# State outputs written as single-value transfers in the middle of a one-core decoder step

## The chip, the core and the metric

One NeuronCore of one Trainium2 chip runs the whole program. The metric is the device time of one execution in microseconds (us), lower is better. Everything is float32 from outside. Inside, each large product is made of three passes over operands split into a high and a low part of TensorE's fast float32 format (fp32r).

## The reference

The program computes one step of a two-branch decoder layer for a prompt of 1024 tokens and 8 single-token samples (1032 columns together):

```python
xn = rms_norm(x, norm_mix)
h, gate_b_in, gate_c_in, u, gate_a, gate_s = jnp.split(xn @ w_in, SPLITS, axis=-1)
conv_y, new_conv_buf = causal_dwconv(gate_c_in * h, conv_buf, conv_a_w, conv_a_b)
z_a = (gate_b_in * conv_y) @ w_out_a
ssm_y, new_re, new_im = s5_mimo(u, s_re, s_im, ...)
ssm_y = jax.nn.gelu(ssm_y)
z_b = (ssm_y @ w_glu_a) * jax.nn.sigmoid(ssm_y @ w_glu_b)
x = x + (jax.nn.sigmoid(gate_a) * z_a + jax.nn.sigmoid(gate_s) * z_b) @ w_o
up_a, up_b = jnp.split(rms_norm(x, norm_ffn) @ w_up, 2, axis=-1)
up_a, new_ffn_buf = causal_dwconv(up_a, ffn_buf, ffn_conv_w, ffn_conv_b)
x = x + (jax.nn.gelu(up_a) * up_b) @ w_down
x = x + jax.nn.sigmoid(rms_norm(x, norm_ple) @ w_ple_gate) * (p @ w_ple)
```

The outputs are `y` (final RMSNorm of `x`, prompt and samples) and the new states: the last two convolution inputs of both convolutions (512 and 2816 channels) and the real and imaginary SSM state (32 groups of 64 values), each for the prompt and for the 8 samples. The model width is 1024, the feed-forward width 2816.

## The kernel before, in words

**Layout.** Activations lie transposed: a tile is 128 channels on the partitions by 1032 tokens. `XT` holds the residual `x` (8 tiles), `XH` and `XL` its scaled high and low parts. A product of one output tile is 72 matmuls of 128x128 by 344 columns: 8 input tiles, 3 passes (`WH`*`XH`, `WH`*`XL`, `WL`*`XH`), 3 column chunks, all in one half of PSUM (`set3(n)` is 3 banks). PSUM banks 6 and 7 are for small work (`bank`, `misc`).

**Staging of weights.** SP loads a 512 KB block into one of two slots of `WST` (`load`, L414) once the split of the block before in that slot is done. ACT copies it to `WH` (`hi`, its engine line is L719), POOL subtracts to `WL` (`lo`, L642), PE waits for `s_wl` (`group`). `hi` waits until PE has finished with the slot's former block.

**Engine programs.** Each engine has an order written out by hand, with semaphores between them; nothing schedules them. In order of time: the start turns `x` (`x_turn`, PE transposes at L1716 into banks 6 and 7, `x_evict` on ACT and DVE) and computes the token norms (`inverse_roots`, `rs_turns` L1754, `rs_evict` L1168); then the projection of `u` (`u_chunk`, `u_product`), the first convolution and the state-space scan; `gate`/`out_a` rounds; eight linear-unit rounds (`glu`, loop at L938 on ACT, each 22.7 us of PE); eight output products (`w_o`, L1496 on DVE adds to `XT`); eleven feed-forward rounds (68 us each); eight rounds of the per-layer embedding (`ple`); the final norm and the output transposes (`out_turn`, L2115).

**States.** DVE leaves the last convolution inputs in `LAST` (128 channels x 26 tiles x 10 values: 2 of the prompt, 8 of the samples; L1402 and L1507) and the SSM state in `FS` (128 x 2 x 16 x 9). Before the change they go out near the end: PE turns them with 58 transposes (`states_out`, L2050 and L2054) in 15 groups, ACT evicts each group to `OST` or `SST`, and SP writes these rows out (L602 to L611).

**End of the feed-forward part.** `down(N_DOWN_END, ...)` adds the last products to `XT` (L1527). DVE has just before that computed `PLW`, the low part of `w_ple` (L1585, L1586). For each new `XT` tile ACT makes `XH` and a square, POOL adds the squares into `RS` (L705), DVE makes `XL` (`split_lo`, L1213). PE runs `product_lo_last` (L1954), in its middle `sum_squares` (L1700: 3 matmuls by a block of ones, which leave every token's sum on all 128 partitions). ACT takes the root of 128x1032 (`rms(2, N_P7)`), DVE the reciprocal (`recip(2)`, L1285), then `ple` scales the first gate product (L1598).

## Time and profile before

| | us |
|---|---|
| three timed executions | 1576.7, 1578.64, 1578.82 |
| their median | 1578.64 |
| the profiled execution | 1578.6 |
| its span in the trace | 1576.8 |
| PE busy in it | 1546.9 (98%) |
| DVE, ACT, POOL busy | 732.8, 418.8, 376.1 |

The profile is one execution. Its span is first to last instruction; 1.8 us lie around it. Matmuls overlap in the pipe, so a matmul's duration is longer than the distance between two of them.

### The profile page before, as it was taken

The numbers are of one execution on the slowest core, as the hardware profiler recorded it, in microseconds if no ns is written. First come the engines' busy times: TensorE is split into PE (matmuls) and PEld (weight loads), VectorE is DVE, ScalarE is ACT, GpSimd is POOL, SyncE is SP. The second block draws the span as 40 slices with busy tenths as digits, with TensorE's granted clock in tenths as the row PEclk, the third lists the DMA queues.
The fourth block names the chain that finished last, engine by engine and source line by source line (L and its number), as shares of the span: only waits on it lengthen the run. The fifth ranks groups of instructions, "written<-read, shape, count | busy, mean of one in ns | idle before, by whom it ended". The sixth has DMA issues, their size and how long they took to land.

```text
span 1576.8 us, 23730 instructions
## 1 busy us (share of the span) xinstructions
PE 1546.9 (98%) x9955; PEld 1528.3 (97%) x9955; DVE 732.8 (46%) x780; ACT 418.8 (27%) x467; POOL 376.1 (24%) x159
## 2 busy tenths in 40 slices
PE   7999999999999999999999999999999999999998
PEld 6899998999999999999999999999999999988998
DVE  4997796233322322245343443534344353458234
ACT  6213212332323222332112121211211112145334
POOL 1121211121212224432213031121313212135241
PEclk9999999999999999999999999999999999999999
DMA  6623617432111103332111020210202111010202
GB/s 183 212 73 102 108 45 190 113 97 79 40 54 53 40 28 120 93 95 81 50 29 57 23 80 2 77 53 27 67 13 80 35 44 53 27 54 0 59 20 108
DMA packets 166499, 108.99 MB, mean 69 GB/s; under 512 B 19217, under 2 KB 158141, under 8 KB 166383
## 3 DMA queue, kind: packets, MB, share of 16 engines
q1 hardware_dynamic: 159794, 99.73, 22.7%
q10 hardware_dynamic: 6656, 8.57, 1.6%
q8 instruction: 36, 0.59, 0.2%
q14 instruction: 13, 0.10, 0.0%
HBM read 89.69 MB, written 17.51 MB: 68 GB/s over the span
## 4 chain that ended last, share of the span: by engine, by line
PE 85%; DVE 9%; DMA 2%; ACT 2%; SPq 1%; issue 1%; ACTq 0%; DVEq 0%
PE PS L1680 60%; PE PS L1980 16%; PE PS L1899 3%; PE PS L1954 1%; DMA sscr<-S 1%; PE PS L2082 1%; SPq L475 1%; PE PS L1852 1%; SPq L463 1%; PE PS L2115 1%; PE PS L1716 0%; PE PS L1842 0%; PE PS L1728 0%; DMA XN<-in_x_prompt 0%; DVE AP L1270 0%
## 5 line engine op out<-in xcount | busy, mean ns | idle before, releaser
L642 POOL TENSOR_TENSOR WL<-WST,WH 128x1024 fp32r<-128x1024 f32 x108 | 266.4, 2467 | 1026.6 <-ACT WH L719 1026.6
L1680 PE MATMUL PS<-XH,WH 128*128 128x344 f32 x1824 | 388.6, 321 | 1.9 <-POOL WL L642 1.3
L1680 PE MATMUL PS<-XL,WH 128*128 128x344 f32 x1824 | 387.0, 320 | 0.0
L1680 PE MATMUL PS<-XH,WL 128*128 128x344 f32 x1824 | 385.0, 319 | 0.0
L1680 PEld LDWEIGHTS PS<-XH,WH 128*128 128x128 f32 x1824 | 305.8, 188 | 2.9 <-POOL WL L642 1.6
L1680 PEld LDWEIGHTS PS<-XL,WH 128*128 128x128 f32 x1824 | 308.5, 189 | 0.0
L1680 PEld LDWEIGHTS PS<-XH,WL 128*128 128x128 f32 x1824 | 304.0, 188 | 0.0
L719 ACT ACTIVATE WH<-WST 128x1024 fp32r<-128x1024 f32 x108 | 110.2, 1021 | 309.0 <-PE PS L1680 238.1
L1527 DVE TENSOR_TENSOR XT<-PS,XT 128x1032 f32<-128x1032 f32 x88 | 108.1, 1230 | 83.0 <-PE PS L1980 83.0
L1980 PE MATMUL PS<-GH,DHW 128*128 128x344 f32 x516 | 110.5, 323 | 3.0 <-DVE XT L1527 3.0
L1980 PE MATMUL PS<-GH,DLW 128*128 128x344 f32 x516 | 109.6, 321 | 0.0
L1980 PE MATMUL PS<-GL,DHW 128*128 128x344 f32 x516 | 109.5, 320 | 0.0
L719 ACT ACTIVATE GH<-TC 128x1032 fp32r<-128x1032 f32 (+1 forms) x24 | 23.9, 994 | 269.6 <-DVE TC L1519 266.5
L1980 PEld LDWEIGHTS PS<-GH,DHW 128*128 128x128 f32 x516 | 86.6, 189 | 3.6 <-DVE XT L1527 3.6
L1505 DVE TENSOR_TENSOR TA<-PS,RS 128x1032 f32<-128x1032 f32 x22 | 27.1, 1232 | 133.8 <-PE PS L1680 133.8
L1290 DVE TENSOR_TENSOR TC<-PS,RS 128x1032 f32<-128x1032 f32 x21 | 25.9, 1232 | 133.1 <-PE PS L1680 133.1
L1980 PEld LDWEIGHTS PS<-GL,DHW 128*128 128x128 f32 x516 | 86.9, 189 | 0.0
L1980 PEld LDWEIGHTS PS<-GH,DLW 128*128 128x128 f32 x516 | 86.7, 190 | 0.0
L719 ACT ACTIVATE TB<-TB 128x1032 f32<-128x1032 f32 x22 | 23.5, 1067 | 124.0 <-DVE TB L1392 124.0
L719 ACT ACTIVATE TB<-TA,KV 128x1032 f32<-128x1032 f32 x22 | 27.6, 1255 | 103.2 <-DVE LAST L1507 103.2
L719 ACT ACTIVATE XH<-XT,KV 128x384 fp32r<-128x384 f32 (+3 forms) x40 | 30.2, 806 | 80.1 <-DVE XT L1496 65.1
L688 POOL TENSOR_TENSOR DLW<-DST,DHW 128x2048 fp32r<-128x2048 f32 x11 | 50.7, 4613 | 0.0
(327 smaller groups left out, 1917.7 us busy)
## 6 DMA issues: line engine op xcount, KB each, us to landing
WST<-in_w_up SPq DMA_DIRECT2D x44, 512.0 KB, 3.9
WST<-in_w_in SPq DMA_DIRECT2D x32, 512.0 KB, 4.5
DST<-in_w_down SPq DMA_DIRECT2D x11, 1024.0 KB, 5.0
xscr<-XT SPq DMA_DIRECT2D x1, 4128.0 KB, 18.4
WST<-in_w_o SPq DMA_DIRECT2D x8, 512.0 KB, 4.4
WST<-in_w_ple_gate SPq DMA_DIRECT2D x8, 512.0 KB, 4.5
out_y_prompt<-OUTT SPq DMA_DIRECT2D x8, 512.0 KB, 2.9
XN<-in_x_prompt ACTq DMA_DIRECT2D x6, 512.0 KB, 8.4
```

Source lines behind the costliest of these rows:

```text
L463: sp.dma_start(U[r * HG:(r + 1) * HG, :, NB:NB + NC], src[:, :, i * NC:(i + 1) * NC]).then_inc(s_ul[q], 16)
L475: sp.dma_start(rows, sscr[q, two * NS:(two + 1) * NS, :, c, :]).then_inc(s_sc[q], 16)
L642: nc.gpsimd.tensor_tensor(WL[:, w], WST[:, slot, 0:tiles * P], WH[:, w].bitcast(F32), ALU.subtract).then_inc(s_wl, 1)
L688: nc.gpsimd.tensor_tensor(DLW[:, :], DST[:, :, :].rearrange("p f n -> p (f n)"), DHW[:, :].bitcast(F32), ALU.subtract).then_inc(s_dl, 1)
L719: copy = lambda o, i, f=ACT.Copy, **k: nc.scalar.activation(o, i, f, **k)
L1290: tt(v3(o), set3(n), v3(RS[:, :]), ALU.mult).then_inc(s_ev, 1)
L1505: tt(v3(TA[:, :]), set3(n), v3(RS[:, :]), ALU.mult).then_inc(s_ev, 1)
L1527: tt(xm, set3(n + m), xm, ALU.add).then_inc(s_ev, 1)
L1680: last = mm(PS[:, 3 * (n % 2) + c, 0:TN], ww[:, w], xx[:, cols], start=(k == 0 and r == 0), stop=(k == ks - 1 and r == 2))
L1852: last = mm(b[two * NS:(two + 1) * NS, c * UC:(c + 1) * UC], W1[:, c, 4 * q + j, two * NS:(two + 1) * NS], UU[q][:, 2 * j + two, 0:UC], st ...
L1899: last = mm(PS[:, 3 * (n % 2) + c, 0:TN], ww[:, w], x[:, c * TN:(c + 1) * TN], start=(k == 0 and r == 0), stop=(k == CT - 1 and r == 2))
L1980: last = mm(PS[:, 3 * (n % 2) + c, 0:TN], ww[:, w], xx[:, k * T + c * TN:k * T + (c + 1) * TN], start=(k == 0 and r == 0), stop=(k == 1 an ...
```

## The change

The new states leave SBUF without a transpose, from ACT's DMA queue, one 4-byte value per piece: `dst` has the channel as its slowest dimension. In each of the eight linear-unit rounds and of the eight output products ACT issues four transfers of SSM state (`states_out(j)`: 128, 1024, 128 and 1024 values); between the two loops, eight transfers of the first convolution (four times 256 and 1024 values); in each feed-forward round four transfers (two times 256 and 1024), and four more after the last one. Together 116 transfers with 70,144 values. The transposes, their evictions and the row writes near the end are gone; two copies of old states within memory stay on SP, behind the load of gate block 3.

Four more edits go with it:

- at the start `x_turn` alternates between banks 6, 7 and banks 2, 5 (`xbank`), so that turn t waits for the eviction of t-2 instead of t-1;
- `inverse_roots()` stands on DVE before the second range-reduction part instead of behind all of them;
- the two `PLW` subtractions come after the additions of down products 1 and 2 instead of before product 0;
- the norm of the last part: `sum_squares` becomes `token_squares` (9 matmuls of one column: 128 tokens on partitions), ACT takes roots of 128x8 and 8x1, DVE reciprocals of the same, PE turns them out to all partitions (`root_turns`, 9 transposes), DVE copies them to `RS`. PE no longer waits for ACT's root before `down_out`. SP's load of the final gain `GFC` is issued before gate block 3 and not behind the state writes.

```diff
+            def states_out(j):
+                for c, part in enumerate(("re", "im")):
+                    for name, cols in ((f"ssm_{part}_p", slice(0, 1)), (f"ssm_{part}_s", slice(1, NB + 1))):
+                        dst = out[name][0].rearrange("b g p -> b (g p)").rearrange("b (j n) -> n j b", n=P)
+                        act.dma_start(dst[:, bass.ds(j, 1), :], FS[:, c, bass.ds(j, 1), cols],
+                                      allow_slow_non_contiguous=True).then_inc(s_so, 16)
+            def last_out(which, f, tile0):
+                for src, cols in ((out[which + "_p"][0, 0], slice(0, 2)), (out[which + "_s"][0, :, 1, :], slice(2, NB + 2))):
+                    rows = src.rearrange("k (f n) -> n f k", n=P)
+                    act.dma_start(rows[:, bass.ds(f, 1), :], LAST[:, bass.ds(tile0, 1), cols],
+                                  allow_slow_non_contiguous=True).then_inc(s_so, 16)
...
                     copy(tile(TH, i * 2 + j), TA[:, :]).then_inc(s_th, 1)
+                    states_out(i * 2 + j)
+
+            for q in range(CT):
+                last_out("conv_a", q, q)
...
                     split_hi(None, tile(XT, m), m, KV[:, bass.ds(m + K_FFN, 1)], TC, i * 2 + (j + 1))
+                    states_out(i * 2 + (j + DT))
...
                 conv_tap(p * 2 + 1)
+                for j in range(2):
+                    last_out("ffn", p * 2 + j, p * 2 + (CT + j))
...
             conv_tap(FT - 1)
+            for f in (FT - 2, FT - 1):
+                last_out("ffn", f, f + CT)
...
-            rms(2, N_P7)
+            act.wait_ge(s_nm, 2)
+            sums = PS[:, 3 * ((N_P7 + 1) % 2), :]
+            copy(SSQ[:, 0, 0:DT], sums[:, 0:DT], ACT.Sqrt, bias=EP[:, :], scale=1.0 / D)
+            copy(SSQ[0:NB, 0, DT:DT + 1], sums[0:NB, DT:DT + 1], ACT.Sqrt, bias=EP[0:NB, :], scale=1.0 / D).then_inc(s_rt, 1)
             hi(G_P7L, 0, N_PW0)
-            for k in range(15):
-                states_out(k)
...
+            if c == 1:
+                inverse_roots()
...
-            dve.wait_ge(s_dh, FP + 1)
-            tt(PLW[:, 0:D], DST[:, 0, :], PHW[:, 0:D].bitcast(F32), ALU.subtract)
-            tt(PLW[:, D:], DST[:, 1, :], PHW[:, D:].bitcast(F32), ALU.subtract).then_inc(s_dl, 1)
             for m in range(DT + 3):
                 if m < DT:
                     down(N_DOWN_END, N_DOWN_END, (m,))
+                if m == 1:
+                    dve.wait_ge(s_dh, FP + 1)
+                    tt(PLW[:, 0:D], DST[:, 0, :], PHW[:, 0:D].bitcast(F32), ALU.subtract)
+                if m == 2:
+                    tt(PLW[:, D:], DST[:, 1, :], PHW[:, D:].bitcast(F32), ALU.subtract).then_inc(s_dl, 1)
...
-            recip(2)
+            dve.wait_ge(s_rt, 2)
+            nc.vector.reciprocal(SSQ[0:NB, 1, DT:DT + 1], SSQ[0:NB, 0, DT:DT + 1])
+            nc.vector.reciprocal(SSQ[:, 1, 0:DT], SSQ[:, 0, 0:DT]).then_inc(s_r7, 1)
+            dve.wait_ge(s_t7, 1)
+            nc.vector.tensor_copy(RS[:, 0:SEQ].rearrange("p (a b) -> p a b", a=2), PS[:, 6:8, :])
+            nc.vector.tensor_copy(RS[:, SEQ:T], PS[:, 3 * (N_P7 % 2) + 2, 400:400 + NB]).then_inc(s_t7, 1)
+            dve.wait_ge(s_t7, 2)
...
-            for k in range(8):
-                states_out(k)
-            rms_read(2)
+            root_turns(N_P7)
             pe.wait_ge(s_dl, FP + 1)
             down_out(N_PW0, N_PW0, 0, PH, PL, PHW, PLW)
-            for k in range(8, 15):
-                states_out(k)
```

**ACT, end of a linear-unit round** (`TH` is the high part of the round's result; the rows behind it are the next round's start or the loop's end). Before:

```order
L719 ACTIVATE TB<-PS 128x1032 [waits s_tf,s_po]
L948 REGISTER_ALU
L719 ISA [waits s_tf]
L719 ACTIVATE TH<-TA 128x1032
L938 REGISTER_ALU
L938 COMPARE_AND_BRANCH
L951 UNCONDITIONAL_BRANCH
L951 ISA
L726 ISA [waits s_stage1]
L719 ACTIVATE WH<-WST 128x1024 [waits s_po]
```

Changed:

```order
L716 ACTIVATE TH<-TA 128x1032
L907 ISA
L907 DMA out_ssm_re_p<-FS 128x1
L907 ISA
L907 DMA out_ssm_re_s<-FS 128x8x1
L907 ISA
L907 DMA out_ssm_im_p<-FS 128x1
L907 ISA
L907 DMA out_ssm_im_s<-FS 128x8x1
L951 REGISTER_ALU
L951 COMPARE_AND_BRANCH
L914 DMA out_conv_a_p<-LAST 128x2x1
```

Four transfers with a register instruction each now stand between the `TH` copy and the next weight copy `WH<-WST`; behind the loop eight more follow (one of them shown) before the `WH<-WST` of the output products.

**PE, from the last low-part matmuls of the first gate product to the second gate product.** Before (the last two groups of the first eight, then `down_out`):

```order
L2050 MATMUL PS<-IDN,LAST 10x128 [waits s_mf]
L2050 MATMUL PS<-IDN,LAST 10x128
L2054 MATMUL PS<-IDN,FS 9x128 [waits s_mf]
L2054 MATMUL PS<-IDN,FS 9x128 x3
L1980 MATMUL PS<-PH,PHW 128x344 [waits s_ev,s_dl,s_rt]
L1980 MATMUL PS<-PH,PHW 128x344 x2
L1980 MATMUL PS<-PL,PHW 128x344 x3
L1980 MATMUL PS<-PH,PLW 128x344 x3
```

Changed:

```order
L1998 MATMUL PS<-XL,WH 128x344 x2
L1745 MATMUL PS<-IDN,SSQ 128x128 [waits s_r7,s_mf]
L1745 MATMUL PS<-IDN,SSQ 128x128 x7
L1747 MATMUL PS<-IDN,SSQ 128x8
L2024 MATMUL PS<-PH,PHW 128x344 [waits s_ev,s_dl]
L2024 MATMUL PS<-PH,PHW 128x344 x2
L2024 MATMUL PS<-PL,PHW 128x344 x3
```

The small transposes of `LAST` and `FS`, each group of which waits for an eviction, are gone; nine transposes of the roots stand in their place, and the wait for `s_rt` has become one for `s_r7`.

**DVE, the end of the feed-forward part.** Before:

```order
L1581 TENSOR_TENSOR TC<-TC,TB 128x344 [waits s_ge,s_ev]
L1583 TENSOR_TENSOR GL<-TC,GH 128x344 [waits s_gh]
L1585 TENSOR_TENSOR PLW<-DST,PHW 128x1024 [waits s_dh]
L1586 TENSOR_TENSOR PLW<-DST,PHW 128x1024
L1527 TENSOR_TENSOR XT<-PS,XT 128x1032 [waits s_po] x4
L1213 SCALAR_TENSOR_TENSOR XL<-XT,KV,XH 128x1032 [waits s_xh]
L1527 TENSOR_TENSOR XT<-PS,XT 128x1032 [waits s_po]
```

Changed:

```order
L1598 TENSOR_TENSOR TC<-TC,TB 128x344 [waits s_ge,s_ev]
L1600 TENSOR_TENSOR GL<-TC,GH 128x344 [waits s_gh]
L1544 TENSOR_TENSOR XT<-PS,XT 128x1032 [waits s_po] x2
L1606 TENSOR_TENSOR PLW<-DST,PHW 128x1024 [waits s_dh]
L1544 TENSOR_TENSOR XT<-PS,XT 128x1032 [waits s_po]
L1608 TENSOR_TENSOR PLW<-DST,PHW 128x1024
L1544 TENSOR_TENSOR XT<-PS,XT 128x1032 [waits s_po]
L1230 SCALAR_TENSOR_TENSOR XL<-XT,KV,XH 128x1032 [waits s_xh]
```

The additions to `XT` of down products 0 and 1 no longer stand behind the two `PLW` subtractions.

## Rows read from the trace of the kernel before

**Rows 1.** The page, part 1: busy time, share, instructions.

```profile
PE 1546.9 (98%) x9955; PEld 1528.3 (97%) x9955; DVE 732.8 (46%) x780; ACT 418.8 (27%) x467; POOL 376.1 (24%) x159
```

**Rows 2.** Chain of waits, 1350 to 1577: start, us, what.

```profile
1410.62 3.32 DVE PLW L1586
...
1434.93 9.65 PE PS L1954 x60
1444.59 1.73 PE PS L1700 x6
1446.32 1.91 PE PS L1954 x12
...
1453.54 2.83 PE PS L1980 x18
...
1460.64 11.36 PE PS L1680 x72
...
1556.34 0.11 PE PS L2102 x2
...
1557.57 0.94 PE PS L2115 x8
```

**Rows 3.** PE's timeline: start, us, what, [idle before, releaser].

```profile
1415.14 0.74 PE L1980 MATMUL PS<-GH,DHW 128*128 128x344 f32 x3 [2.71 <-DVE XT L1527]
```

**Rows 4.** Stretches: us; PE, PEld, DVE, ACT, POOL; granted clock, DMA share, GB/s.

```profile
1416.00:1418.00 2.00, 2.00 (x10) 2.00 (x9) 0.23 (x1) 2.00 (x3) 0.00 (x0) 0.55 0.00 0
1420.00:1422.00 2.00, 2.00 (x15) 2.00 (x14) 1.05 (x1) 0.92 (x1) 1.72 (x1) 1.00 0.00 0
```

**Rows 5.** PE's timeline, the start.

```profile
36.36 0.87 PE L1716 MATMUL PS<-IDN,XS 8*128 8x8 f32 x8 [0.33 <-ACT XT L719]
...
47.53 1.09 PE L1754 MATMUL PS<-IDN,SSQ 128*128 128x128 f32 x8 [1.75 <-DVE SSQ L1164]
```

**Rows 6.** Chain of waits at the start.

```profile
48.22 1.29 DVE RS L1168 x2
```

**Rows 7.** Timeline of a linear-unit round, then of the change to the output products.

```profile
451.51 1.07 ACT L719 ACTIVATE TH<-TA 128x1032 f32 x1 [8.63 <-DVE TA L1485]
...
455.03 2.40 POOL L642 TENSOR_TENSOR WL<-WST,WH 128x1024 fp32r<-128x1024 f32 x1 [15.31 <-ACT WH L719]
...
458.67 0.63 PE L1680 MATMUL PS<-YGH,WH 128*128 128x344 f32 x3
...
587.63 1.07 ACT L719 ACTIVATE TH<-TA 128x1032 f32 x1 [8.63 <-DVE TA L1485]
...
589.73 2.58 POOL L642 TENSOR_TENSOR WL<-WST,WH 128x1024 fp32r<-128x1024 f32 x1 [12.99 <-ACT WH L719]
...
595.10 1.23 DVE L1496 TENSOR_TENSOR XT<-PS,TA 128x1032 f32 x1 [5.04 <-PE PS L1680]
```

**Rows 8.** DVE's timeline behind the feed-forward part.

```profile
1431.26 2.43 DVE L1213 SCALAR_TENSOR_TENSOR XL<-XT,KV,XH 128x1032 fp32r<-128x1032 f32 x1
...
1447.51 6.60 DVE L1285 RECIPROCAL RS<-RS 128x1032 f32<-128x1032 f32 x1 [1.16 <-ACT RS L719]
```

**Rows 9.** The `GFC` load (1024 values): its issue, and the DMA view of 1469.0 to 1470.85.

```profile
1468.76 0.41 SPq L613 DMA_DIRECT2D GFC<-in_norm_final  x1
...
DMA packets 1107, 0.04 MB, mean 21 GB/s; under 512 B 1040, under 2 KB 1107, under 8 KB 1107
...
q1 hardware_dynamic: 1107, 0.04, 37.0%
```

**Rows 10.** Issue durations of one line: min/median/max ns (L510: 1024 pieces of 512 B).

```profile
L778 ACTq DMA_DIRECT2D uscr<-US x4: 455/826/1365, 52.4 to 91.2; - x4
...
L510 SPq DMA_DIRECT2D WC<-w2scr x4: 1817/2183/2565, 182.1 to 188.6; - x4
```

**Rows 11.** ACT's timeline near 52: engine work and a DMA issue.

```profile
51.95 1.06 ACT L719 ACTIVATE WH<-WST 128x1024 fp32r<-128x1024 f32 x1 [5.02 <-PE PS L1728]
52.03 0.38 ACTq L777 DMA_DIRECT2D uscr<-TA  x1
```

More of the change, by code:

```diff
@@ L153, in decoder_step @@
         SQA = at("SQA", [P, T], B0)
-        GFC = at("GFC", [P, DT], B0 + TB4)
-        RT = at("RT", [P, 2, 12], B0 + TB4 + 32)
+        GFC = at("GFC", [P, DT], E0 + 4 * TB4 + 26144)
+        RT = at("RT", [P, 2, 12], E0 + 4 * TB4 + 26176)
         XN = at("XN", [P, DT, D], B0)
@@ L271, in decoder_step @@
         s_rt = sem("s_rt")
+        s_r7 = sem("s_r7")
+        s_t7 = sem("s_t7")
         s_dv = sem("s_dv")
@@ L350, in bank, with xbank @@
             return PS[:, 6 + k % 2, :]
+        def xbank(t, half):
+            return PS[:, ((6, 7), (2, 5))[t % 2][half], :]
         def out_banks(t):
@@ L757, in x_evict @@
                 act.wait_ge(s_xt, 2 * t + 1)
-                copy(X3[:, 0:4, t * P:t * P + w], bank(0)[:, :].rearrange("p (m t) -> p m t", t=P)[:, :, 0:w]).then_inc(s_xe[0], 1)
+                copy(X3[:, 0:4, t * P:t * P + w], xbank(t, 0)[:, :].rearrange("p (m t) -> p m t", t=P)[:, :, 0:w]).then_inc(s_xe[0], 1)
             def split_x(c):
@@ L1704, in rms_read, with token_squares, root_turns @@
                 pe.wait_ge(s_rt, count)
+            def token_squares(n, tiles):
+                pe.wait_ge(s_ev, n)
+                pe.wait_ge(s_acc, tiles)
+                for t in range(DT + 1):
+                    cols = slice(t * P, min(t * P + P, T))
+                    last = mm(PS[0:P if t < DT else NB, 3 * ((n + 1) % 2), t:t + 1], RS[:, cols], ONES[:, 0:1], start=True, stop=True)
+                last.then_inc(s_nm, 1)
+            def root_turns(n):
+                pe.wait_ge(s_mf, M_OUT)
+                pe.wait_ge(s_r7, 1)
+                for t in range(DT):
+                    tr(PS[:, 6 + t // 4, (t % 4) * P:(t % 4 + 1) * P],
+                       SSQ[:, 1, t:t + 1].to_broadcast([P, P]), IDN[:, :])
+                tr(PS[:, 3 * (n % 2) + 2, 400:400 + NB], SSQ[0:NB, 1, DT:DT + 1].to_broadcast([NB, P]),
+                   IDN[0:NB, 0:NB]).then_inc(s_t7, 1)
             def x_turn(t):
@@ L1710, in x_turn @@
                 for half in range(2):
-                    if t:
-                        pe.wait_ge(s_xe[half], t)
+                    if t >= 2:
+                        pe.wait_ge(s_xe[half], t - 1)
                     for m in range(4):
@@ L1715, in x_turn @@
                         src = XN[:, t, f] if t < DT else XS[:, f]
-                        last = tr(bank(half)[:, m * P:m * P + w], src, IDN[0:w, 0:w])
+                        last = tr(xbank(t, half)[:, m * P:m * P + w], src, IDN[0:w, 0:w])
                     last.then_inc(s_xt, 1)
```

52 lines of the change are left out of this document (13 added, 39 removed).

## The prediction

> **What bounds it now.** I read the page's first part for the busy times, then the chain of waits, then windows and timelines of the few places where PE is not busy. PE is busy for 1546.9 of 1576.8 us [rows 1], so a change pays only where PE stands still or does work that can go, and it costs where a later `WL`, `XL` or `ev` reaches PE. From 300 to 1400 us PE has no gap. The one weak stretch is the end of the feed-forward part: DVE computes `PLW` (3.32 us for its second half) [rows 2] while PE, done with down products 0 and 1, waits 2.71 us and restarts at 1415.14 [rows 3]. Behind this pause the granted clock is 0.55, near the lower of the two levels (1.2 and 2.4 GHz), and it is back at 1.00 from 1420 on [rows 4]. Then the chain runs over 1434.93 (first gate product), 1444.59 (sum of squares) and 1448.23 (end of the 1.91 us of low-part matmuls), and the second gate product starts only at 1460.64 [rows 2]. Between the last two lie the 58 transposes with their 15 evictions and one 2.83 us `down_out`.
>
> **Start.** PE waits 0.33 us on ACT's eviction of the turn before [rows 5] and about as much at five other turns behind column chunk 0. With four banks these waits go: about 0.65 us for each of the two later groups of three turns, 1.3 together. The reciprocal comes late because DVE has other small work first: PE waits 1.75 us for it [rows 5]. The edit removes that wait, but the other small work then stands behind it and before the copies to `RS` [rows 6], so the products that follow gain only some 0.3. All that follows up to 285 us hangs together (DVE, PE and transfers), so I carry **1.6 us** on. Bounds: 0.3 (DVE and the loads take it all back) and 2.5.
>
> **The `PLW` edit.** DVE adds down product 0 as soon as it is there, about 1410.9 to 1412.1; PE goes on at 1412.4 without a pause, and keeps its clock. DVE then has: addition 1 (1.23, the price of the like addition in rows 7) to 1413.5, the first `PLW` half to 1414.8, addition 2 to 1416.4, the second half to about 1418.3, addition 3 to 1419.5. From here a step is one addition and one `XL` of 2.43 [rows 8], 3.5 us with its waits, against 2.83 of PE [rows 2], so DVE paces: additions 4 to 7 end at 1423.4, 1426.9, 1430.4 and 1433.9. PE's next product waits for addition 6 and starts at 1430.4 instead of 1434.93: 4.5 us earlier. Its high part takes 7.6 (the 9.65 of rows 2 hold twelve low-part matmuls, 2.0, more), so the low part starts at 1438.0.
>
> **The norm.** Three matmuls by ones cost 1.5 net of the pipe (1.73 in the chain) [rows 2]. The nine one-column matmuls resemble the six between 1556.34 and 1557.57, 0.205 each [rows 2], so 1.85. Low part to 1439.9, sums to 1441.75, low part done at 1443.6. By then `XL` 7 (DVE, three more of about 2.1 behind 1436.1) is there at 1442.2, the small roots and reciprocals at about 1442.8. Root turns: 1.09 for eight [rows 5] and 0.2 for the ninth, to 1444.9. After that two strands run beside each other: PE's `down_out`, 2.83; DVE's copies, 1.29 [rows 6] and 0.16, with the scaling of 1.23 and semaphores, about 3.1. The second gate product starts at **1448.0 instead of 1460.64: 12.6 us earlier**, of which 4.6 come from before the low part ends and 8 from the transposes and evictions. DVE's 6.60 us reciprocal [rows 8] leaves the path. Bounds: 9 us if every step of DVE meets POOL and drags, 14.5 if PE paces and not DVE. What follows is PE work of the old length. The copies within memory and `GFC` have 10 us of cover.
>
> **The 116 transfers.** Price of issuing one: 0.41 for 1024 single values, but into SBUF [rows 9]; 0.455 at the least and 1.37 at the most for 128 pieces of 32 bytes out of SBUF on ACT's queue; 2.18 for 1024 pieces of 512 bytes that queue up behind one another [rows 10]. I take 0.46, since the count of pieces is that of `GFC` and the direction that of `uscr<-US`; the ends are 0.4 and 2.2. A transfer is issued while ACT still works on what stands before it: `uscr<-TA` at 52.03 beside the `WH` copy of 51.95 [rows 11].
> - Linear-unit rounds: `TH` at 451.51, `WL` ends at 457.43, PE needs it at 458.67 [rows 7]. Four issues end at 453.35; table load, `WH` copy and `WL` then end at 458.2. No cost, 0.4 us of room. Three of the rounds are like this, the other four within the loop have no table load and 2.3 us of room instead of 1.2.
> - Between the loops: `TH` at 587.63, `WL` done at 592.3, needed at about 594.9 [rows 7]. Twelve issues end at 593.1, the `WH` copy at 594.2, `WL` at 596.8: PE waits 1.9. SP issues four loads at the same time, so I take **2.5 us**, ends 0.9 and 13.
> - Output products: four issues fit under the `XH` copy and the square. Feed-forward rounds: 0.8 us later for a weight copy that has over 3 us of room, and the gelu waits 4 us for DVE anyhow. Last round: four issues beside DVE's convolution. Nothing each. If this cover went, it would cost 0.8 us a round.
> - DMA engines: 1107 packets, 1040 of them small, took 37.0% of 16 engines for 1.85 us, 9.9 ns each [rows 9]. 70,144 values are 43 us per engine out of 1577; 2304 of them delay a weight load by 1.4 us, and loads have 5 us and more of room. The twelve transfers are 7424 values, 4.6 us, less than their issue.
>
> On this last point the Trainium skill speaks against the change: "DMA: Bandwidth & Descriptors", Specifications, has transfers below 512 B done as read-modify-write. The only row on 4-byte pieces [rows 9] writes to SBUF, so no trace here shows the price in memory. If that doubled the time of a packet, the twelve transfers would last 9 us and hold ACT's queue back by some 4 us more; the sum would then be 1571 by that page.
>
> **Sum**, against the profiled execution's 1578.6 (the median of the runs is 1578.64, so they agree): -1.6 - 12.6 + 2.5 = -11.7, so **1567.0**.
>
> **Rivals.** (a) *The issue price is ACT's undoing.* ACT's sequencer is blocked while a transfer of 1024 pieces is taken in, 2.18 us as for `WC<-w2scr` and 0.61 for a short one. A linear-unit round then has 5.6 us of issues: late by 3.3 in three rounds and by 2.2 in four, and the twelve transfers last 16.7, late by 13.2. 1578.6 - 14.2 + 9.9 + 8.8 + 13.2 is **1596**. It decides from about 0.55 us per issue in the loop, and equals no change near 0.95. For it: [rows 10], and that both queues share the engines. Against: `WC` had 2 MB of loads and small pieces before it, here the engines are a tenth to a fifth busy. (b) *Half of that*: about 1 us per issue. Loop rounds late by 1.7 and 0.5, the transition by 8.4: 15.5 in all, **1580**. (c) *The end of the feed-forward part stays DVE's*: the pause moves into later steps, POOL and DVE slow each other throughout, the norm saves only the evictions: 8 us instead of 12.6 and nothing at the start, **1573**. (d) *PE paces everywhere and the transition costs nothing*: -1.6 - 14.5, **1562.5**. That the change does not do what it says would be values that still leave late, behind the y output; but the last of them is issued at about 1399, 170 us before the end, so I give that nothing.
>
> **Chances.** Forecast 0.60; (c) 0.15; (d) 0.08; (a) 0.08; (b) 0.09. The range reaches from (d) to above (c) and into the bound of the transition: 1561.5 to 1576, and leaves out (a) and (b). A measurement of this kernel can tell about 0.2% (3 us) from no change. Faster by more: 0.83; within: 0.06; slower: 0.11.
>
> **What would show it.** Right: PE's second gate product 12 to 13 us closer to the start of the last down products; no pause of over 1 us before down product 2, and the clock at 1.00 there; no `L2050` or `L2054`; issues on ACT's queue of about 0.46 us; one new wait of PE on `WL` of 2 to 3 us at the first output product, none in the linear-unit rounds; packets up by 70,000. Wrong: issues over 0.6 us, PE waiting for `WL` in every other linear-unit round, or a granted clock below 1 after the transition's pause. The forecast falls if the 1024-value transfers take longer to issue than the 128-value ones.

## The result: 1797 to 1824 us where 1567 was forecast, and the profile after

The changed kernel took 1820.91 us (median of 5 runs, 1796.87 to 1824.4), against 1578.64 for the kernel before on the same chip: ratio 1.148, 95% interval 1.142 to 1.155. The ratio leaves out the two executions of the changed kernel (1824.29 and 1824.4) that lie over 1.5% above its fastest. The prediction had 1567.0 with a range up to 1576.0 and gave "slower" a chance of 0.11. The median lies 254 us above the forecast. Every count below is made on the profiled execution of 1796.87.

The page of the changed kernel (part 1, then the rows of 40 slices for the granted clock and the DMA engines, then the queues; q1 is SP's, q10 is ACT's):

```profile
PE 1574.3 (88%) x9918; PEld 1551.8 (86%) x9918; DVE 694.8 (39%) x783; ACT 410.6 (23%) x453; POOL 375.6 (21%) x159
PEclk9999999999888885778879999999999999999999
DMA  6623564323977767999987516515516326423102
DMA packets 238422, 108.99 MB, mean 61 GB/s; under 512 B 91178, under 2 KB 230102, under 8 KB 238334
q1 hardware_dynamic: 159718, 99.45, 41.1%
q10 hardware_dynamic: 78656, 8.86, 11.2%
```

PE is busy for 27 us more than in [rows 1], though it has 37 instructions less, and stands still for 220 instead of 30. The packets rose by 71,923, where 70,000 were forecast. What was not forecast is the share of q1: SP's 159,718 packets with 99.45 MB now come to 41.1% of the 16 engines' span, where the same packets come to 22.6% in the run `e1_none` below. Such a share, and the DMA share of the stretches below, adds up the times of packets. It can pass 1 (1.11 and 1.25 in two stretches of the run `i1_scratch_outlay` below), so packets of one engine overlap in it, and it holds waiting as well as work.

Where the time went is plain from stretches of the changed kernel (us; PE, PEld, DVE, ACT, POOL busy; granted clock, DMA share, GB/s):

```profile
0.00:427.00 427.00, 408.64 (x2729) 397.52 (x2730) 263.05 (x379) 133.40 (x185) 85.71 (x53) 1.00 0.44 115
427.00:700.00 273.00, 185.41 (x1056) 179.97 (x1054) 44.40 (x37) 44.95 (x42) 34.06 (x15) 0.85 0.73 26
700.00:1000.00 300.00, 192.53 (x1106) 189.26 (x1107) 64.18 (x52) 45.94 (x43) 62.17 (x23) 0.81 0.87 51
1000.00:1400.00 400.00, 400.00 (x2538) 400.00 (x2537) 151.02 (x154) 74.66 (x66) 87.81 (x30) 1.00 0.44 47
```

Up to the first transfer at 427 nothing is lost. Then the DMA share is 0.73 to 0.87 at only 26 to 51 GB/s, and PE stands still for 195 us. The mean granted clock is 0.85 and 0.81 of the higher level (2.4 GHz): it is at the lower one (0.50, 1.2 GHz) within long pauses and for some us behind them, as from 683 to 735. PE is busy for 34 us more than in `e1_none`, and with the 195 that is the whole 230 between the two. The feed-forward rounds carry their single values without a loss: PE has no gap from 1000 to 1400 even at a DMA share of 0.44.

The first linear-unit round with transfers, in the timeline of the changed kernel:

```profile
427.34 0.39 ACTq L907 DMA_DIRECT2D out_ssm_re_p<-FS  x1
427.90 0.40 ACTq L907 DMA_DIRECT2D out_ssm_re_s<-FS  x1
428.46 0.47 ACTq L907 DMA_DIRECT2D out_ssm_im_p<-FS  x1
429.10 0.39 ACTq L907 DMA_DIRECT2D out_ssm_im_s<-FS  x1
...
433.37 0.37 SPq L417 DMA_DIRECT2D WST<-in_w_glu_b  x1
...
433.84 10.22 SPq L417 DMA_DIRECT2D WST<-in_w_glu_a  x1
...
445.16 11.73 SPq L417 DMA_DIRECT2D WST<-in_w_in  x1
```

The four issues cost 0.39 to 0.47 us each, close to the 0.46 that the prediction took, and those of 1024 values are no longer than those of 128. Here it is SP's loads behind them that stick: the issue of the second one lasts 10.22 us. Windows of the same place have a DMA share of 1 and more with hardly a byte moving:

```profile
443.00:450.00 7.00, 6.71 (x32) 6.42 (x33) 0.00 (x0) 1.03 (x1) 0.00 (x0) 0.78 1.17 15
450.00:454.00 4.00, 4.00 (x28) 4.00 (x27) 1.70 (x2) 0.00 (x0) 0.00 (x0) 1.00 1.00 9
```

At the change to the output products ACT's own queue is stuck (timeline of the changed kernel):

```profile
675.51 12.79 ACTq L914 DMA_DIRECT2D out_conv_a_p<-LAST  x1
679.56 52.72 SPq L417 DMA_DIRECT2D WST<-in_w_o  x2
...
692.19 26.46 ACTq L914 DMA_DIRECT2D out_conv_a_p<-LAST  x1
...
728.22 1.06 ACT L716 ACTIVATE WH<-WST 128x1024 fp32r<-128x1024 f32 x1 [55.89 <-issue]
...
731.95 1.20 PE L1705 MATMUL PS<-TH,WH 128*128 128x344 f32 x3 [53.37 <-POOL WL L639]
```

The twelve issues that the prediction counted as 5.5 us last from 671.44 to 727.96, and PE waits 53.37 us for `WL`. The `WH` copy before that `WL` starts 0.26 us after the last issue has ended: ACT was blocked by its own issues, and its row names no load. SP's row puts two issues into one. The first lasts 9.64 us, the second 0.38 from 731.89 on, behind the `WH` copy; most of the 52.72 is SP's wait for the slot and not a stuck queue.

The output products show the same on ACT, and the waits of ACT from 427 to 920 us show both ways of the loss (us in total, times, longest):

```profile
749.78 15.03 ACTq L907 DMA_DIRECT2D out_ssm_im_p<-FS  x1
...
766.01 1.06 ACT L716 ACTIVATE WH<-WST 128x1024 fp32r<-128x1024 f32 x1 [16.05 <-issue]
```

```profile
ACT WH L716 <- issue: 140.5, 8, 55.9
ACT WH L716 <- DMA WST<-in_w_in: 55.1, 4, 18.1
...
ACT L716 <- DMA WST<-in_w_glu_a: 34.5, 3, 17.9
```

Of PE's 195 us, five waits with 95.7 us in all (the 53.37 and four of 5.17 to 16.24 from there to 900) stand behind a `WH` copy that starts within 0.5 us of the end of ACT's last issue; seven waits of 3.48 to 15.03 us, 70.3 in all, stand behind a copy that waited for a load. So the linear-unit rounds lose by SP's late loads, and the transition and most of the output products by ACT's blocked issues.

The last part is as forecast in kind. PE's timeline, then the chain of waits, of the changed kernel:

```profile
1637.82 0.42 PE L2051 MATMUL PS<-GH,DHW 128*128 128x344 f32 x1 [1.17 <-DVE TC L1591]
...
1658.00 0.74 PE L2024 MATMUL PS<-GH,DHW 128*128 128x344 f32 x3 [0.42 <-DVE XT L1544]
1661.41 0.71 PE L1998 MATMUL PS<-XH,WH 128*128 128x344 f32 x3 [0.30 <-issue]
```

```profile
1671.09 1.80 PE PS L1737 x18
1672.89 2.09 PE PS L1998 x12
1674.98 0.88 PE PS L1745 x8
...
1679.03 11.36 PE PS L1705 x72
```

The pause of 2.71 us [rows 3] is gone. From the down tail at 1637.82 to the first gate product are 23.59 us, to the second 41.21; before, the same tail began at 1407.92 and the two followed after 27.01 and 52.72 [rows 2]. So the other edits gained 3.4 and 8.1 us here. At the start `TH` of the first linear-unit round ends its wait at 427.14 instead of 428.83, but this place moves from one execution to the next: in the 18 profiled executions with the new start it lies between 425.10 and 429.29, with a median of 427.9. The transfers lost about 230.

### The profile page after: what moved, and what is told of

The parts are those of the page before. It is cut to its first block, busy times and chain, and to the rows that moved or that the text cites. A ratio compares the mean times of both kernels' runs of the same rounds, so it can differ in the third digit from the quotient of the medians.

```text
span 1794.8 us, 23964 instructions
## 1 busy us (share of the span) xinstructions
PE 1574.3 (88%) x9918; PEld 1551.8 (86%) x9918; DVE 694.8 (39%) x783; ACT 410.6 (23%) x453; POOL 375.6 (21%) x159
## 3 DMA queue, kind: packets, MB, share of 16 engines
q1 hardware_dynamic: 159718, 99.45, 41.1%
q10 hardware_dynamic: 78656, 8.86, 11.2%
## 4 chain that ended last, share of the span: by engine, by line
PE 56%; issue 33%; DVE 3%; POOL 3%; ACTq 1%; ACT 1%; another core or an unknown queue 1%; DMA 1%; SPq 0%; POOLq 0%; DVEq 0%
PE PS L1705 36%; PE PS L2024 14%; POOL WL L639 2%; PE PS L1787 1%; ACTq L907 1%; DMA WST<-in_w_in 1%; PE PS L1998 1%; PE PS L2110 1%; PE PS L1896 1%; POOL RS L646 0%; PE PS L1772 0%; PE PS L2143 0%; PE PS L1886 0%; DVE XL L1230 0%
## 5 line engine op out<-in xcount | busy, mean ns | idle before, releaser
L639 POOL TENSOR_TENSOR WL<-WST,WH 128x1024 fp32r<-128x1024 f32 x108 | 261.8, 2424 | 1265.5 <-ACT WH L716 1251.1
L1705 PE MATMUL PS<-XH,WH 128*128 128x344 f32 x1824 | 392.8, 324 | 40.8 <-POOL WL L639 18.4
L1705 PE MATMUL PS<-XH,WL 128*128 128x344 f32 x1824 | 388.9, 321 | 8.4 <-issue 8.4
L716 ACT ACTIVATE WH<-WST 128x1024 fp32r<-128x1024 f32 x108 | 110.6, 1024 | 626.8 <-issue 158.5
L1705 PE MATMUL PS<-TH,WH 128*128 128x344 f32 x192 | 46.4, 354 | 95.9 <-POOL WL L639 95.9
L1705 PEld LDWEIGHTS PS<-TH,WH 128*128 128x128 f32 x192 | 36.4, 213 | 97.5 <-issue 97.5
L1705 PE MATMUL PS<-YGH,WH 128*128 128x344 f32 x192 | 45.3, 345 | 41.9 <-POOL WL L639 39.4
L1705 PEld LDWEIGHTS PS<-YGH,WH 128*128 128x128 f32 x192 | 35.3, 207 | 46.1 <-issue 25.5
```

The costliest lines, as they stand in the source:

```text
L639: nc.gpsimd.tensor_tensor(WL[:, w], WST[:, slot, 0:tiles * P], WH[:, w].bitcast(F32), ALU.subtract).then_inc(s_wl, 1)
L716: copy = lambda o, i, f=ACT.Copy, **k: nc.scalar.activation(o, i, f, **k)
L1705: last = mm(PS[:, 3 * (n % 2) + c, 0:TN], ww[:, w], xx[:, cols], start=(k == 0 and r == 0), stop=(k == ks - 1 and r == 2))
```

## The experiments

Seventeen kernels ran, each beside the kernel before, in the order below except that runs which belong together stand together. Theories by letter: **A**, each small piece costs engine time whatever it is; **B**, each transfer costs, by its issue; **C**, single values that lie side by side in memory hinder one another on the way to it; **D**, small writes to the outputs' memory are slow; **E**, how the values lie sets the price, the distance of a transfer's rows included. A' and D' in the expectations are A and D as the runs before had left them.

### Without the transfers

```diff
-                    states_out(i * 2 + j)
...
-                last_out("conv_a", q, q)
...
-                    last_out("ffn", p * 2 + j, p * 2 + (CT + j))
```

> The changed kernel without its 116 single-value transfers; the rows of the states are not written, which is left out of the work. Theory: the loss of 218 us lies in the transfers alone, and the other edits gained what the trace of the changed kernel shows at its two ends, 1.7 us before the first linear-unit round and 11.5 + 0.4 from the last down product of the feed-forward part to the end. Then 1578.6 - 13.6 = 1565.0 us (1563 to 1567), the granted clock at 1.00 from 400 to 700 us, under-512-byte packets back near 19,000. Rival: the four-bank turns or the moved constants upset something in the middle as well; then over 1575.

Measured: 1566.67 us (5 runs), ratio 0.9927, interval 0.9914 to 0.9941. The granted clock is 1.00 from 427 to 1000 us and PE has no gap there. The whole loss lies in the transfers, and the rest of the change gains 11.5 us (3.4 and 8.1 in the last part, as above; `TH` ends its wait here at 428.38). Nothing in the middle was upset.

### Fewer pieces, fewer transfers

Whole partitions into scratch memory, with the 116 transfers kept:

```diff
-                        act.dma_start(dst[:, bass.ds(j, 1), :], FS[:, c, bass.ds(j, 1), cols],
+                        act.dma_start(fscr[:, c, bass.ds(j, 1), cols], FS[:, c, bass.ds(j, 1), cols],
```

> All 116 transfers at the same places with the same bytes, but into scratch memory laid out by channel, so that each partition writes its 8 (or 1, or 2) values as one piece: 128 pieces a transfer, 14,848 instead of 70,144. The rows of the states are not written in the outputs. Theory A (each piece occupies a DMA engine for about 120 ns, worked out from 10,496 values that raised the engines' share over 300 us of feed-forward rounds from 0.15 to 0.41): a linear-unit round holds 512 pieces, 4 us of 16 engines instead of 17, and the weight loads keep up: 1565 to 1575. Theory B (what costs is a transfer, by its issue or its set-up, whatever its pieces): as slow as the changed kernel, over 1700.

Measured: 1571.8 us. And only the prompt's states, as in the changed kernel:

```diff
-                    for name, cols in ((f"ssm_{part}_p", slice(0, 1)), (f"ssm_{part}_s", slice(1, NB + 1))):
+                    for name, cols in ((f"ssm_{part}_p", slice(0, 1)),):
```

> Only the 58 transfers of the prompt's states (128 or 256 values each), in place of 116: the sample's states are not written. 4096 + 6656 values of 70,144. Theory A (by the piece): 256 pieces a linear-unit round, 2 us of the engines, hidden: 1565 to 1570. Theory B (by the transfer): half of the loss stays, near 1680.

Measured: 1596.04 us, where A had 1570 and B 1680. Both theories fall: 10,752 single values cost 29 us over `e1_none`, 14,848 pieces (half of them 32 bytes, half 4 or 8; within a transfer over 1000 bytes from one to the next) cost 5, with twice the transfers. In `e3_few` the loads crawl behind only 256 values a round; the DMA view of its stretch from 427 to 450 us (40 slices; engines' share, GB/s) has them at 12 to 59 GB/s for some 9 us before they go at 300:

```profile
DMA  0001000000023605655869926929083214998410
GB/s 0 0 1 1 0 0 0 0 0 0 0 66 111 57 0 4 59 16 20 18 33 15 20 24 16 49 49 37 12 21 20 37 16 110 297 325 236 126 33 21
```

What sets the slow pieces apart is that they are 4 bytes and lie side by side: that became theory C.

### The same transfers elsewhere in time

```diff
                 for j in range(2):
                     last_out("ffn", p * 2 + j, p * 2 + (CT + j))
+                if states:
+                    states_out(p * 2)
+                else:
+                    for j in range(2):
+                        last_out("conv_a", p * 2 + (j - NJ), p * 2 + (j - NJ))
...
+                if states:
+                    states_out(p * 2 + 1)
```

> The changed kernel with all single-value transfers of the scan's states and of the first convolution moved into the feed-forward rounds: two tiles of the states a round in the first eight, two of the convolution a round in the next two, beside the two of the feed-forward convolution that are there already. Theory A: 7168 values a round are 53 us of the engines, loads 10 more, of 68 us; the linear-unit rounds and output products are whole again, and the loads of the rounds, each slowed by the values ahead of it, arrive just in time or late by some us: 1565 to 1620. Rival (the loads of the feed-forward rounds have no room for more than they carry now): the 230 us come back there, near 1790.

Measured: 1770.07 us (4 runs), ratio 1.123, interval 1.118 to 1.128. Neither number was quite hit, the rival's (1790) was nearer. The linear-unit rounds are whole (PE busy 273.00 of 273 us from 427 to 700), the feed-forward rounds lose instead, at a DMA share of 0.82 and 34 GB/s. The cost goes with the transfers, and the room of the feed-forward rounds ends between 2560 and 7168 values a round. By the queues' shares in this run (q1 33.5 and q10 21.2% of 16 times 1771.3 us, less those of `e1_none`) a value adds 131 ns of packet time, its effect on the loads included, and a round of 7168 values 59 us on each engine; with 10 of loads that is about the whole round of 68.

### The distance between values

Now every value has a place of its own, k floats from the next, in scratch memory. Count, order, queue and places in the program are those of the changed kernel.

```diff
+        fscr = nc.dram_tensor("fscr", [2, NJ, NB + 1, P, k], F32, kind="Internal").ap()
+        lscr = nc.dram_tensor("lscr", [CT + FT, NB + 2, P, k], F32, kind="Internal").ap()
...
-                        dst = out[name][0].rearrange("b g p -> b (g p)").rearrange("b (j n) -> n j b", n=P)
+                        dst = fscr[c, :, cols, :, 0].rearrange("j b n -> n j b")
```

k = 16, 128, 8, 4, 2 and 1:

> The changed kernel with its 116 transfers of 70,144 single values at the same places, but each value goes to a scratch place of its own, 64 bytes from the next, in place of next to its neighbour. The rows of the states are not written in the outputs. Theory C (what costs is that single values beside one another in memory are written at the same time: 512 pieces a round at distances of 32 bytes and more cost 5 us in all, 256 pieces a round beside one another cost 30 and slowed the loads to 20 GB/s): the loss goes, at most 9.9 ns for each piece, 43 us of engine time spread over the kernel, 1565 to 1585. Theory A' (the count of pieces of 4 bytes costs, wherever they go): as slow as the changed kernel, about 1800.

> The same with 512 bytes from one value to the next. Theory C with a unit of 64 bytes or less: the same time as at a distance of 64 bytes. Theory C with a unit of up to 512 bytes: fast here and slow there. Theory A': about 1800 at both distances.

> As the runs with 64 and 512 bytes between single values (1578.4 and 1579.0 us), with 32 bytes. Theory C with a unit of 32 bytes or less: 1578. With a unit of 64 bytes two values share one: slower, though with two sharers and not sixteen, 1590 to 1700.

> The same with 16 bytes between single values. Unit of 32 bytes: two values share one and the loads slow down, between 1590 and 1750. Unit of 16 bytes or less, or only values that touch one another collide: 1578.

> The same with 8 bytes from one value to the next. At 16 bytes the time was 1581.7, 3 above that at 32 to 512. Theory C: the loss lies between the two, and where it lies tells how the price grows with the number of values that share a stretch; by a doubling of the excess at each halving of the distance, 1585 to 1590; by a threshold at 8 bytes, over 1700. Theory D: 1580.

> As the runs with 16 to 512 bytes between single values, with no room between them: 70,144 single values side by side, in scratch memory and not in the outputs. Theory C (single values side by side collide): as slow as the changed kernel, 1750 to 1820. Theory D (small writes to the outputs' memory are slow, whatever their distance; every fast run so far wrote to scratch): about 1578.

| bytes from value to value | time, us | ratio, interval |
|---|---|---|
| 512 | 1579.02 | 1.0009, 0.9998 to 1.0019 |
| 64 | 1578.4 | 1.0003, 0.9993 to 1.0013 |
| 32 | 1578.86 | 1.0003, 0.9993 to 1.0013 |
| 16 | 1581.67 | 1.0017, 1.0007 to 1.0027 |
| 8 | 1590.64 | 1.0076, 1.0050 to 1.0102 |
| 4 (dense) | 1631.13 | 1.0337, 1.0307 to 1.0367 |

The queues of the runs at 64 bytes and dense, by their pages (packets, MB, share of 16 engines):

```profile
q1 hardware_dynamic: 159718, 99.45, 22.9%
q10 hardware_dynamic: 78656, 8.86, 4.0%
```

```profile
q1 hardware_dynamic: 159718, 99.45, 32.1%
q10 hardware_dynamic: 78656, 8.86, 8.1%
```

With the packet counts of the changed kernel, to the packet, the time is 1578 to 1579 at 32 bytes and more, and rises below: by 3, 12 and 52 us. Theory A is out: the same 70,144 values cost 12 us over `e1_none` when they are apart. Theory C holds in scratch in its sign, but its number for the dense run (1750 to 1820) was far too high. There is no sharp step: each halving of the distance makes the rise some four times as large. It is not a matter of two values in one stretch of 64 or 512 bytes, since 32, 64 and 512 agree; a stretch of 32 bytes would fit, but no run shows which part has it. The packets' times tell the two parts of the price. q10's share over `e1_none` (1.6% of 16 times 1564.7 us) comes to 8.4 ns a packet at 64 bytes (4.0% of 16 times 1576.8, less that, by 72,000 packets: 70,144 values and 16 more for each transfer), 24 ns dense. The larger part is SP's: its unchanged loads take 5777 us of packet time at 64 bytes and 8366 dense.

In the first round at 64 bytes the transfers are issued the same way and SP's queue does not notice them (timeline of this run):

```profile
428.42 2.19 ACTq L910 DMA_DIRECT2D fscr<-FS  x4
434.49 0.37 SPq L420 DMA_DIRECT2D WST<-in_w_glu_b  x1
434.95 0.46 SPq L420 DMA_DIRECT2D WST<-in_w_glu_a  x1
439.27 0.37 SPq L420 DMA_DIRECT2D WST<-in_w_in  x1
```

The two loads that took 10.22 and 11.73 us to issue take 0.46 and 0.37.

These runs also show what the transfers cost when no value lies beside another, which the prediction had put at 2.5 us for the transition. Timelines of ACT and PE in the run at 64 bytes:

```profile
589.18 2.34 ACTq L910 DMA_DIRECT2D fscr<-FS  x4
591.69 8.93 ACTq L917 DMA_DIRECT2D lscr<-LAST  x8
600.88 1.06 ACT L719 ACTIVATE WH<-WST 128x1024 fp32r<-128x1024 f32 x1 [10.81 <-issue]
```

```profile
604.60 1.20 PE L1708 MATMUL PS<-TH,WH 128*128 128x344 f32 x3 [8.28 <-POOL WL L642]
```

The first four issues are 0.6 us apart, the eight behind them 1.1 on average, with one of 3.54, and PE waits 8.28 us. With 128 pieces a transfer (`e2_wide`) none of the twelve lasts over 0.67 us and PE waits 3.47, so the count of pieces costs here even when they are apart.

### Pieces side by side, and whose memory

> The 58 transfers of the sample's states as 128 pieces of 32 bytes that lie beside one another in scratch memory (no room between them), the 58 of the prompt's states as pieces of 4 or 8 bytes 64 bytes apart. The rows of the states are not written in the outputs. Theory C with a unit of 32 bytes or less: 1565 to 1573. With a unit of 64 bytes and more two to sixteen pieces share it, and the loads slow down as they did for 4-byte neighbours: over 1590. Theory A': 14,848 pieces, as in the run with whole-partition pieces, 1572.

Measured: 1570.44 us (`fscr` as `[2, NJ, P, NB]`, each partition's 8 values one piece, the pieces touching). Pieces of 32 bytes may touch; 4-byte ones may not. But up to this run every kernel that lost much had written to the outputs, and every one that kept the transfers and lost little had written to scratch, so memory and layout were crossed (first the line of the changed kernel, then that of the run):

```diff
-                        dst = out[name][0].rearrange("b g p -> b (g p)").rearrange("b (j n) -> n j b", n=P)
+                        dst = (out[name][0].rearrange("b g p -> (b g p)").rearrange("(j n b) -> j n b", n=P, b=NB) if cols.stop > 1 else fscp[c, :, :, 0:1]).rearrange("j n b -> n j b")
```

> As the run with 32-byte pieces side by side in scratch (1570.4 us), with the 32 transfers of the sample's scan states writing their pieces into the output arrays of these states, in an order that is not the outputs'. The values of these outputs are in wrong places, and the other states are not written to the outputs. Theory C: 1570. Theory D: 4096 pieces in outputs' memory slow the loads, over 1590.

Measured: 1571.39 us. Writes of 32 bytes to the outputs' memory are not slow as such; single values apart from one another were not tried there. Then the outputs' layout, but in scratch (arrays of the outputs' shapes as the destination):

> The changed kernel with its transfers of single values at the same places, into scratch arrays that have the shapes of the outputs, so that the 8 sequences' values of a channel lie 4 to 22 KB apart and not 512 bytes as in the dense scratch run (1631 us). The rows of the states are not written in the outputs. Theory E (the layout sets the rest of the price: values side by side and the rows of a transfer far apart): as slow as the changed kernel, 1780 to 1820. Theory D' (the outputs' memory makes the rest): 1631.

Measured: 2137.77 us (2 runs, 2124 and 2151), ratio 1.354. And the dense run's layout, but in the outputs, for the sample's scan states:

```diff
-                        dst = out[name][0].rearrange("b g p -> b (g p)").rearrange("b (j n) -> n j b", n=P)
+                        dst = (out[name][0].rearrange("b g p -> (b g p)").rearrange("(j b n) -> j b n", n=P, b=NB) if cols.stop > 1 else fscr[c, :, cols, :, 0]).rearrange("j b n -> n j b")
```

> As the dense scratch run (1631 us), with the 32 transfers of the sample's scan states (32,768 single values) into the output arrays of these states, in the dense run's order: rows of 128 values side by side, 512 bytes apart. The values of these outputs are in wrong places, and the other states are not written to the outputs. Theory E: 1631. Theory D': most of the way to the changed kernel, over 1720.

Measured: 1670.0 and 1696.4 us, two runs only and without an interval. Neither theory gave these numbers. The same shapes in scratch cost 560 us instead of 240, so the outputs' memory is not what makes the changed kernel slow, and going from rows 512 bytes apart to rows 4 to 22 KB apart raises the price of dense values from 52 us to hundreds in these runs (theory E in sign, far off in size). But arrays of one shape at two places differ by some 300 us (the two kernels were not run on one chip; the kernel before takes 1578.33 and 1578.64 us beside them), and the dense layout takes at least 39 us more with these states in the outputs (1670.0 against 1631.13). The page of `i1_scratch_outlay`:

```profile
q1 hardware_dynamic: 159718, 99.45, 51.9%
q10 hardware_dynamic: 78656, 8.86, 17.3%
```

Distance between rows alone is harmless in scratch: at 64 bytes between values the rows of a transfer lie 8 KB apart too, as the sample's scan states do in the outputs, and the time is that of 32 and 512 bytes. It takes values side by side as well. On what in an address the rest depends was not tried and stays open.

### The two edits at the end, each put back

On top of `e1_none`, both halves of `PLW` before the eight additions:

```diff
+            dve.wait_ge(s_dh, FP + 1)
+            tt(PLW[:, 0:D], DST[:, 0, :], PHW[:, 0:D].bitcast(F32), ALU.subtract)
+            tt(PLW[:, D:], DST[:, 1, :], PHW[:, D:].bitcast(F32), ALU.subtract).then_inc(s_dl, 1)
             for m in range(DT + 3):
```

> The kernel without transfers of single values, with both halves of PLW back in front of the eight down additions; the rows of the states are not written. The traces of the two kernels put this edit at 3.4 us (27.0 against 23.6 us from the down tail of the feed-forward part to the next product). Then 1566.7 + 3.4 = 1570.1; by the prediction's own sum, 4.5, 1571.2; if DVE catches up during the product, 1567.

Measured: 1569.6 us (5 runs), ratio 0.9944, interval 0.9930 to 0.9958: 2.9 us by the medians, and PE's wait of 2.71 is back at 1414.42. By the trace 3.4. The two intervals overlap, but every run of this kernel (from 1568.88) is above every one of `e1_none` (to 1567.35).

```diff
-            copy(SSQ[:, 0, 0:DT], sums[:, 0:DT], ACT.Sqrt, bias=EP[:, :], scale=1.0 / D)
...
+            rms(2, N_P7)
...
-            root_turns(N_P7)
+            rms_read(2)
```

> The kernel without transfers of single values, with the old norm of the third part (three matmuls by ones, square root and reciprocal of 1032 values on every partition), and without the old 58 transposes; the rows of the states are not written. If the 8 us lay in the transposes and their evictions alone, the 6.60 us reciprocal and the square root have PE's 2.8 us and little else beside them once the transposes are gone, and come out on the path: low part end, square root of about 1.2, reciprocal 6.6, scaling 1.2, against 3.8 from the sums to the second gate product now: 1566.7 + 3 to 6, about 1571. Rival: hidden, 1567.

Measured: 1572.58 us (5 runs), ratio 0.9960, interval 0.9947 to 0.9974: 5.9 us slower than `e1_none`. Its chain of waits, then PE's timeline:

```profile
1442.91 1.13 ACT RS L716
...
1444.07 6.61 DVE RS L1290
...
1450.70 1.24 DVE TA L1605
```

```profile
1452.08 1.20 PE L1687 MATMUL PS<-XH,WH 128*128 128x344 f32 x3 [4.49 <-DVE TA L1605]
```

Without the transposes the 6.61 us reciprocal ends on the path. The 5.9 us have two parts. The second gate product starts 44.17 us after the down tail (1407.91 to 1452.08), against 41.21 with the small norm: 3.0. And behind the pause of 4.49 us the granted clock is 0.50 until 1457, so that this product takes 14.07 us instead of 11.36: 2.7. Taking the transposes away alone thus brings the product forward by 5.1 of the 8.1 us, and gives about half of that back by the slower clock.

### A version that beats both

The states leave without 4-byte writes to memory and without PE. ACT writes `FS` and `LAST` to scratch as they lie; SP fetches single values back into rows in SBUF that are free at the time (behind `GH` and `GL` during the feed-forward rounds, in the place of `DHW` and `DLW` in the tail), and writes the rows out.

```diff
+            act.dma_start(fscr, FS[:, :, :, :]).then_inc(s_fw, 16)
...
+            def gather_states(j):
+                for c in range(2):
+                    sp.dma_start(RA[c * (NB + 1):(c + 1) * (NB + 1), bass.ts(j, P)],
+                                 fscr[:, c, bass.ds(j, 1), :].rearrange("n j b -> b (j n)"),
+                                 allow_slow_non_contiguous=True).then_inc(s_ga, 16)
...
+                sp.dma_start(RB[:, t * P:(t + 1) * P], lscr[:, t:t + 1, :].rearrange("n t k -> k (t n)"),
+                             allow_slow_non_contiguous=True).then_inc(s_gb, 16)
```

> The other edits kept, and the states sent out without single-value writes to memory and without transposes: ACT writes the two state buffers to scratch memory as they lie (128 pieces of 1152 and of 1040 bytes), SP then fetches them back in single values (70,144 of them, 32 transfers of 1152 in the feed-forward rounds and 26 of 1280 in the tail) into rows in SBUF, and ten contiguous row transfers write the outputs. All outputs are written. Theory C: single values cost 9.9 ns each when they are read from memory and written to SBUF, 4.3 us of all engines for 6912 values a feed-forward round, hidden: 1565 to 1570, faster than both kernels. Theory A' (single values slow the loads in any direction): the loads of the feed-forward rounds and the tail are late, over 1600.

Measured: 1564.65 us (4 runs, 1563.92 to 1568.09), ratio 0.9923, interval 0.9906 to 0.9940: 12 us faster than before. (The 6912 values a round of the expectation are 4608.) The queue SP's loads and fetches share, by the page of this run:

```profile
q1 hardware_dynamic: 230486, 100.01, 26.7%
```

The share was 22.6% without the fetches; 70,768 packets more added 1015 us of packet time, 14 ns each, and PE has no gap from 427 to 1400. The time is that of `e1_none`, so the states now leave at no cost that these runs can tell. Reading single values from memory and writing them to SBUF is as cheap as [rows 9] said.

## Why the prediction was wrong, by its own steps

- **"DMA engines: ... 9.9 ns each ... loads have 5 us and more of room."** This is the step that failed. The price came from the one row on 4-byte pieces [rows 9], which reads memory and writes SBUF, and was carried to writes into memory side by side. The prediction said in its next paragraph that no trace showed that price, and then kept 9.9 ns in the sum and no bound above it in the range. Measured: 9.9 ns is about right where the direction is the same (14 ns in `f4_rows`) and even for writes into memory that lie apart (8.4 ns). In the outputs' layout it was 39 ns a packet (11.2% of 16 times 1794.8 us, less `e1_none`'s share, by 72,000), which is 5.6 us of 16 engines for a round's 2304 values and still not the main part: the loads' own packets took 6100 us more of packet time. The step priced the transfers' own time on the engines and never what they do to the packets of others, nor what late engines do to the next issue.
- **Weighed against the Trainium skill.** The page "DMA: Bandwidth & Descriptors", Specifications, calls transfers below 512 B read-modify-writes, and the prediction drew 1571 from it. (The doubled packet time behind that number was the prediction's own assumption.) The page speaks of the size of a transfer, and size alone does not tell these runs apart: all pieces here are far below 512 B, yet values 32 bytes apart cost what values 512 bytes apart do, and 32-byte pieces that touch are cheap. The page's warning pointed the right way, and its sign deserved a rival with a chance of its own.
- **Issue price, 0.46 us.** Right where nothing is stuck (0.36 to 0.47). The prediction's own test, that it "falls if the 1024-value transfers take longer to issue than the 128-value ones", did not catch the failure: the longest issues of scan states are 15.52 us for 128 values and 9.47 for 1024. Its other signs of being wrong did show: issues over 0.6 us, PE waiting for `WL` in linear-unit rounds, and a granted clock below 1 behind the transition's pause. That an issue waits for the transfers ahead of it in the queue fits these rows; no run isolates it.
- **Transition, +2.5.** Mis-sized: 8.3 us even without collisions (twelve issues, 11.4 us instead of 5.5), within its bounds of 0.9 and 13. Values apart leave the kernel at 1578, no gain: the transfers, this wait above all, take back the 12 us that the other edits gained. In the real layout PE's wait here was 53, outside the bounds, and it came from ACT's blocked issues.
- **Linear-unit rounds and output products, 0.** Wrong: with the transition between them PE stood still for 195 us. **Feed-forward rounds, 0.** Right, at 2560 values a round, though their loads are slowed as well: ACT waits up to 12.4 us for one between 1100 and 1200 us, and PE still has no gap.
- **Start, -1.6.** The 1.7 of this one execution is luck as far as the runs tell: the median of all executions with the new start is 0.9 ahead of the one profile of the kernel before, and they spread over 4 us. The reciprocal's wait of 1.75 is gone, as said (0.25 now), but PE then waits 3.33 us for DVE at 50.30.
- **`PLW` edit, -4.5.** 3.4 by the trace, 2.9 by the run with it undone. DVE paces as forecast; its second subtraction takes 3.30 us, as long as in [rows 2], where the working had 1.9; POOL is busy for 3.45 of the 4 us beside it.
- **Norm, -8.** 8.1, but the reason was in part wrong. Of "8 from the transposes and evictions", 5.1 come without the small norm and 3.0 need it; in time the small norm is worth 5.9, since without it a pause also costs clock. The run with the old norm shows both.
- **Rivals.** None named the mechanism. (a), blocked issues, had one of the two ways of the loss: ACT's copies late behind its own issues, at the transition above all. It put this at 32 us where PE's waits of this kind are 95.7, by the count of pieces in a transfer and not by what is stuck ahead, and it left out SP's late loads. The sum without the transfers, 1578.6 - 14.2 = 1564.4, against 1566.67 measured, was good. (The terms of the forecast itself add up to 1566.9.)

## What to carry to other kernels

Price a transfer by where its pieces land, and ask what it does to the packets of other queues, not only what it costs itself: single 4-byte writes to memory side by side held up the issue of 256 and 512 KB loads by 10 us and more, at a small share of the bytes, and the engine that issued them stood blocked in front of its own copies for up to 55.89 us. When values must be turned round on their way out, write them as they lie, fetch them singly into SBUF and send rows. When a term rests on a row of another direction, the range has to show it.

## What the runs showed of the hardware

- 4-byte writes into memory: no dearer at 32 bytes from one to the next than at 512 (1578.9 and 1579.0 us, 12 above the kernel without them), costlier from 16 bytes down (1581.7, 1590.6, 1631.1 dense), and far costlier when the dense rows of one transfer lie kilobytes apart (1797 to 1824 and 2138 us for the same shapes at two places in memory). 32-byte pieces may touch (1570.4 and 1571.4).
- They cost the reads of another queue more time in all than themselves: 159,718 load packets took 35 ns each without them (22.6%) and 74 ns with them (41.1%). Few packets carry this. Counted over the packets of the trace, the median of the 512-byte load packets is 27 ns in `e1_none` and in the changed kernel alike; there 3263 of 125,604 take 500 ns or more (17 in `e1_none`), and these are 4376 of 8841 us. The median of the 4-byte packets on ACT's queue stays at 9 ns too.
- While they are under way an issue can take long on either queue: up to 11.73 us for a load on SP and 26.46 for 256 values on ACT, where the same loads take 0.37 to 0.46 to issue in the run at 64 bytes.
